# Adaptive-norm tables and S5 tables of a hybrid decoder step computed between the tiles of its first projection

## What is computed

```python
# adaLN: shift, scale and gate vectors from the conditioning row (9 rows: 1 prompt, 8 samples)
mod = jax.nn.silu(c) @ w_ada + b_ada            # (9,1024) @ (1024, 6*1024); w_ada_final: (1024, 2*1024)
sh1, sc1, gt1, sh2, sc2, gt2 = jnp.split(mod, 6, axis=-1)
h = rmsnorm(x, g_norm1) * (1.0 + sc1) + sh1     # x: 1088 tokens x 1024
proj = h @ w_in                                 # u is its first 512 columns; then q, k, v, forget gate
...
# S5, a diagonal complex state-space model over u: 32 groups of 16 channels, 64 states each
a = exp(lambda * dt); bb = f(a, lambda) * b
h_t = a * h_{t-1} + bb u_t;  y_t = Re(c h_t) + d u_t
...
# then attention, the output projection, and a mixture of experts (64 experts, top 6)
```

## Time and profile before

| | us |
|---|---|
| median of three runs (lowest, highest) | 2054.55 (2053.19, 2056.24) |
| the profiled execution, its own time | 2055.19 |
| the span that its trace covers | 2053.5 |
| PE busy in the span | 1815.0 (88%) |
| DVE busy | 851.8 (41%) |
| ACT busy | 451.1 (22%) |
| POOL busy | 218.3 (11%) |
| HBM read / written | 336.11 MB / 63.75 MB |

### The profile page before, as it was taken

The page is one execution under the profiler, slowest core; times in us unless marked ns, Lnnn a source line. Parts: engine busy times, 40 slices in busy tenths (PEclk is TensorE's granted clock), DMA queues, the critical chain, the costliest instruction groups (busy, mean ns, idle before and its releaser), DMA issues.

```text
span 2053.5 us, 25239 instructions
## 1 busy us (share of the span) xinstructions
PE 1815.0 (88%) x8920; PEld 942.0 (46%) x8920; DVE 851.8 (41%) x2392; ACT 451.1 (22%) x859; POOL 218.3 (11%) x183
## 2 busy tenths in 40 slices
PE   4568878999988887789888889999999999999985
PEld 1146555454445555455464334444444444444442
DVE  4943471003156555222236234344344434434438
ACT  0122213100044443130342111111111111111122
POOL 0000001000010000400000012222222222222210
PEclk7679958999978888899988989999999999999998
DMA  7932023000201003730017279999999999999666
GB/s 275 371 96 79 25 77 137 0 0 0 82 9 42 1 1 125 267 134 0 1 62 210 72 305 368 373 372 381 381 371 377 380 376 349 354 379 374 210 171 259
DMA packets 108585, 402.95 MB, mean 196 GB/s; under 512 B 27568, under 2 KB 38484, under 8 KB 78749
## 3 DMA queue, kind: packets, MB, share of 16 engines
q1 hardware_dynamic: 89452, 332.13, 42.2%
q0 software_dynamic: 19008, 69.21, 12.8%
HBM read 336.11 MB, written 63.75 MB: 195 GB/s over the span
## 4 chain that ended last, share of the span: by engine, by line
PE 47%; issue 6%; DVE 2%; DMA 1%; ACT 1%; POOL 0%; SPq 0%; POOLq 0%; DVEq 0%; ACTq 0%
PE psum L1033 22%; PE psum L1044 11%; PE psum L885 6%; PE psum L1012 3%; PE psum L1051 1%; PE psum L915 1%; PE psum L921 1%; PE psum L911 1%; PE psum L963 1%; PE psum L928 1%; DVE arena L1754 1%; DMA arena<-h_rows,arena 0%; DVE arena L1740 0%; DVE arena L1742 0%; DMA arena<-moe_rows 0%
## 5 line engine op out<-in xcount | busy, mean ns | idle before, releaser
L1033 PE MATMUL psum<-arena 128*32 128x512 f32 (+2 forms) x2016 | 464.4, 597 | 1.1 <-ACT arena L2019 1.1
L1033 PEld LDWEIGHTS psum<-arena 128*32 128x32 f32 (+2 forms) x2016 | 169.7, 139 | 241.7 <-issue 239.8
L1044 PE MATMUL psum<-arena,tail 128*32 128x512 f32 (+2 forms) x1000 | 231.6, 595 | 0.0
L1686 DVE TENSOR_TENSOR arena<-arena,psum 128x256 f32<-128x256 f32 x65 | 39.6, 609 | 339.4 <-ACT arena L2024 336.4
L2161 POOL DMA_INDIRECT moe_rows<-arena x64 | 101.6, 1588 | 576.0 <-DVE arena L1714 437.6
L1044 PEld LDWEIGHTS psum<-arena,tail 128*32 128x32 f32 (+2 forms) x1000 | 80.1, 138 | 105.1 <-issue 105.1
L703 PE MATMUL psum<-arena 128*128 128x512 f32 (+1 forms) x384 | 126.9, 494 | 0.0
L885 PE MATMUL psum<-arena 128*128 128x512 f32 (+1 forms) x288 | 124.3, 594 | 0.5 <-ACT arena L1950 0.5
L2024 ACT ACTIVATE arena<-psum 128x256 f32<-128x256 f32 x65 | 24.9, 383 | 445.0 <-PE psum L1033 445.0
L744 PE MATMUL psum<-arena 128*128 128x512 f32 (+2 forms) x192 | 89.9, 586 | 13.6 <-ACT arena L1868 13.6
L885 PEld LDWEIGHTS psum<-arena 128*128 128x128 f32 (+1 forms) x288 | 68.7, 239 | 54.8 <-issue 39.4
(11 more groups left out here) (488 smaller groups left out, 2251.0 us busy)
## 6 DMA issues: line engine op xcount, KB each, us to landing
arena<-in_w_exp_gate SPq DMA_DIRECT2D x66, 1024.0 KB, 19.2
arena<-in_w_exp_up SPq DMA_DIRECT2D x66, 1024.0 KB, 24.6
arena<-in_w_exp_down SPq DMA_DIRECT2D x66, 1024.0 KB, 21.6
arena<-in_w_ada SPq DMA_DIRECT2D x12, 2048.0 KB, 8.8
arena<-in_w_ada_final SPq DMA_DIRECT2D x4, 2048.0 KB, 8.5
arena<-in_cache_k SPq DMA_DIRECT2D x32, 256.0 KB, 4.4
arena<-in_cache_v SPq DMA_DIRECT2D x32, 256.0 KB, 3.9
arena<-moe_rows SPq DMA_DIRECT2D x16, 512.0 KB, 11.4
```

Source lines behind the costliest of these rows:

```text
L1033: ins = pe.matmul(slot[2 + par][lo:hi, :].rearrange("p (u n) -> p u n", u=2), xTs[:, par, k, lo:hi], gu, start=(k == 0), stop=(k == KD - 1))
L1044: ins = pe.matmul(slot[1][lo:hi, n * 512:(n + 1) * 512], hTs[:, k, lo:hi], down_ring[at][:, k * D + n * 512:k * D + (n + 1) * 512], start= ...
```

## The change

- Only the first adaLN group (pieces 0 to 3) and piece 4 are computed ahead of the u projection. Pieces 5 and 6 follow the transposes of tile 0, piece 7 the projection that is made in tile 1's turn, then 8, and one piece each (9 to 15) follows the projections in the turns of tiles 2 to 8. All groups now use PSUM slot 5, and all their transposes slot 4. The turns of groups 1, 2 and 3 stand in tile 1's turn, in tile 5's turn and behind the last projection.
- ACT's copies and bias additions of groups 1 to 3 stand between its norm and copy work of the tiles. The two sines of the rotation table now come behind the last of them.
- On DVE the two complex products are cut into halves of three operations each, and stand in the turns of tiles 1 to 4; the angles are cut into three parts in the turns of tiles 5 to 7. The scale `a1` is made ahead of the tiles, with only group 0 waited for; `a2` and `af` come after the skip term.
- BS and K come after UT on PE, and their copies after UT's on DVE. The DMAs of `M` come after them, so behind all loads of x and behind the eight small DMAs of the sample rows.
- The loads of x are interleaved with those of the weight pieces in SP's queue.
- ACT waits for `M`'s DMAs at the copy of S group 14, and no longer at the first tile of `u`. DVE waits for UTS ahead of writing the first states.
- Several arena offsets move (`u`, `u8`, `sq_junk`, `skip`).

The core of the diff, PE first:

```diff
+            ada_piece(0)
+            turn_parameters()
+            for n in range(1, NPIECE):
+                ada_piece(n)
+            turn_mod(0)
+            ada_piece(NPIECE)
...
+            for t in range(NT):
+                pe.wait_ge(xn_ready, t + 1)
+                fill(pe, ("X", t), t % 2)
...
+                full(ins, ("X", t))
+                if t == 0:
+                    ada_piece(5)
+                    ada_piece(6)
+                if t:
+                    project_u(t - 1)
+                    ada_piece(PIECE_AT[t])
+                if t == 1:
+                    ada_piece(8)
+                    turn_mod(1)
+                if t == 5:
+                    turn_mod(2)
+            project_u(NT - 1)
+            turn_mod(3)
```

DVE's loop over the tiles, then ACT's:

```diff
                     modulate(("X", t - 1), t - 1, slot[(t - 1) % 2], lambda k, t_=t - 1: tile_of(hT, t_, k), a1, lambda k: mod_t[:, k])
+                if t in (1, 2):
+                    output_table(t - 1)
+                elif t in (3, 4):
+                    input_table(t - 3)
+                elif t in (5, 6, 7):
+                    angles(t - 5)
```

```diff
-                    if t == 0:
-                        act.wait_ge(toeplitz, 16 * CH)
...
+                if t == 3:
+                    mod_out(1)
+                if t == 7:
+                    mod_out(2)
+                if t == 2:
+                    mod_copy(1)
                 if t >= 2:
                     u_out(t - 2)
+                if t == 5:
+                    mod_copy(2)
             u_out(NT - 2)
+            mod_copy(3)
             u_out(NT - 1)
+            mod_out(3)
...
                 full(act, ("S", gp))
+                if gp == 14:
+                    act.wait_ge(toeplitz, 16 * CH)
```

SP's queue (`load_x(t)` waits for the transposes of tile t-2):

```diff
+            for n in range(2, 5):
+                load_ada(n)
+            dma(w_u, ap["w_in"][0][:, 0:DA].rearrange("(k p) n -> p k n", p=P)).then_inc(ld["wu"], 16)
+            load_ada(5)
+            load_ada(6)
+            load_x(2)
+            for n in range(7, 9):
+                load_ada(n)
+            load_x(3)
+            load_ada(9)
+            load_ada(10)
+            for t in range(4, NT):
+                load_x(t)
+                load_ada(t + 7)
```

More of the change, by code:

```diff
@@ L565, in turn_mod @@
                 slots.wait_empty(pe, ("ADA", g))
-                fill(pe, ("ADT", g), 4 + g % 2)
+                fill(pe, ("ADT", g), 4)
                 for i in range(4):
-                    ins = pe.transpose(slot[4 + g % 2][:, i * P:(i + 1) * P], mod_row[:, g % 2, i * P:(i + 1) * P], ident)
+                    ins = pe.transpose(slot[4][:, i * P:(i + 1) * P], mod_row[:, g % 2, i * P:(i + 1) * P], ident)
                 full(ins, ("ADT", g))
[L571 to L586, removed]
@@ L587, in _, with ada_piece @@
-            turn_mod(NADG - 1)
+            def ada_piece(n):
+                g, q = divmod(n, NPIECE)
+                if q == 0:
+                    fill(pe, ("ADA", g), 5)
+                pe.wait_ge(ld_ada[n % 2], 16 * (n // 2 + 1))
+                for k in range(q * KPER, (q + 1) * KPER):
+                    for j in range(4):
+                        ins = pe.matmul(slot[5][32 * j:32 * (j + 1), :], cs_t[:, k, :], ada_w[:, n % 2, k % KPER, j * 512:(j + 1) * 512], start=(k == 0), stop=(k == KD - 1))
+                if q < NPIECE - 1:
+                    ins.then_inc(ada_used, 1)
+                else:
+                    full(ins, ("ADA", g))
@@ new lines, in _, with project_u @@
+            ada_piece(0)
[4 more added lines that the diff above has]
+            ada_piece(NPIECE)
+            def project_u(t):
+                slots.wait_empty(pe, ("X", t))
+                if t == 0:
+                    pe.wait_ge(ld["wu"], 16)
+                fill(pe, ("U", t), 2 + t % 2)
+                for k in range(KD):
+                    ins = pe.matmul(slot[2 + t % 2][0:rows(t), :], tile_of(hT, t, k), w_u[:, k, :], start=(k == 0), stop=(k == KD - 1))
+                full(ins, ("U", t))
@@ L590, in _ @@
+            project_u(NT - 1)
+            turn_mod(3)
+            slots.wait_empty(pe, ("U", 7))
+            for q in range(8):
+                fill(pe, ("UT", q), 4 + q % 2)
+                for i in range(4):
+                    ins = pe.transpose(slot[4 + q % 2][:, i * P:(i + 1) * P], u[:, 4 * q + i].rearrange("p t i -> p (t i)"), ident)
+                full(ins, ("UT", q))
             pe.wait_ge(s5_mats, 2)
```

178 lines of the change are left out of this document (88 added, 90 removed).

## The result

The changed kernel takes 1995.01 us, the median of four runs (1994.54 to 1997.38), against 2054.58 of the kernel before (2053.19 to 2056.24): 59.6 us less. The ratio worked out from the single runs is 0.9718, 95% interval 0.9697 to 0.9739 (the quotient of the two medians is 0.9710). Its profiled execution took 1995.10 us, with a span of 1993.4.

A forecast was written before the change was run, and what follows sets the result against it. The opening up to the first Y was bound by a weight-waiting and a PE-bound stage in sequence; its parts summed to Y at 208.2 instead of 258.43, 50.2 us less, giving 2004.3 us, range 2001 to 2018.

The forecast's parts named there:

- Part 2: Tile 1's turn, through tile 2's transposes: 17.0 us, ending at 84.7, with transposes at 1.84 and first projection 8.92.
- The bound: Opening up to first Y: a weight-waiting stage, then a PE-bound one, stand one after the other; first Y at 258.43.
- Part 1: Start up to weight piece 6: nothing changes, and piece 6 ends at 67.7.
- The upper bound of 13.6: First projection in tile 1's turn if wholly at the low clock; upper end of its -2 to +4.7 us.
- Part 3: Tiles 2 to 8: DVE sets the pace, PE's turn being 9.8; modulation of tile 7 ends at 146.7, PE at 163.4.
- Part 4: Ahead of UT: PE waits for ACT's group 3 bias additions, 2.64 and 0.1; UT starts at 166.2.
- Part 5: Behind the tiles: UT 5.7, BS 6.8, K 11.31 ending at 190.0, S to Y 15.59; Y starts at 208.2.
- the patchy clock: Rival: in the tiles' turns the high clock comes and goes, lengthening projections by 2.6; 2014 us, chance 0.17.
- Late weights: Rival: weight pieces inside the tiles' turns land late again, only piece 9 showing, +3; 2007 us, chance 0.04.
- the low clock throughout: Rival: interleaved tiles and pieces keep PE at 1.2 GHz, turns of 19.1; 2081 us, slower, chance 0.03.
- `M` was last: Rival: ahead of Y, the last `M` DMA lands after 7.7, ready at 211.9; 2008 us, chance 0.06.
- the sign that I had named: At the first Y: release by ACT's copy of S group 14 would show the forecast wrong.

The follow-up runs named there:

- turn_angles_late: turn_late with the last third of DVE's angles moved from tile 7's turn to behind the last modulation; ratio to the kernel before 0.9715.
- turn_late: The changed kernel with group 3's turn moved from ahead of UT to behind it; ratios to the kernel before 0.9698 and 0.9714.
- weights_first: The changed kernel with all weight pieces, their copies and turns ahead of the tiles again, x loads behind them; ratio to the kernel before 1.0093.
- after_delay1: The changed kernel with SP's first DMA held back by one GpSimd memset of 3.5 us; ratio to the kernel before 0.9751.

## Why the prediction was right and where it failed

The kernel took 1995.0 us for 2004.3 forecast. What failed is a size in two places, and not the mechanism. The transposes of tile 1 and the first projection (Part 2) were put at 10.76 us and took 8.24. And the difference that one run has from another was put at nothing: S took 7.68 us and not 9.10, and the part behind Y came out 4 us shorter, with attention's extent.

**The bound, and that two stages could share one stretch: right.** The first Y products stand in this order: 275.0 with only the tables between the tiles, 258.4 before, 250.6 with only the weights, 242.2 with neither (BS, K and `M` behind), 202.4 with all. Counted from 242.2, the weights alone cost 8.4 us, the tables alone 32.8, and both together gain 39.8. Neither part is good by itself, with BS, K and `M` behind the tiles in all four: DVE's tables and the weight stream must run at the same time as each other, as they did before, and the tiles must run beside both.

**Part 1: right**, 67.4 for 67.7 (66.0 and 67.4 in the other two traces of the changed kernel: in one of them piece 6 took 1.92).

**Part 2: the term that was mis-sized.** I took tile 1's transposes at 1.84 and the first projection at 8.92, both from tiles 0 and 1 of the kernel before, where PE had been idle ahead of them (3.78 and 1.12). In the changed kernel pieces 5 and 6 run right up to them, and they took 1.09 and 7.15. That is 2.5 of the 3.1 us of this step; the rest is overlap at the joints of PE's stages, which I had counted at full length. In all eight traces in which pieces and tile 1's transposes ran right up to the first projection it took 7.15. In the four in which PE had been idle shortly before (3.78 to 6.58 us, then tile 0's and tile 1's transposes, then another 1 us) it took 8.92, 7.26, 9.37 and 7.26. I had named 7.0 as the lower bound of this term, -2, and it came. Piece 7 in the earlier trace rows had shown the high clock behind two pieces, but the eight pieces after it in that trace took 2.62 to 3.64, each behind an idle span; what should have moved the forecast is that the change takes these spans away. (The upper bound of 13.6 doesn't follow from the words beside it: 3.64 for four steps is 0.91 a step, so 14.6 for sixteen. No run shows a projection wholly at the low clock.)

**Part 3: right in each term and in its end; the pace in between was PE's.** The turns of DVE were 14.4, 11.0, 12.2, 11.1 and 9.9 against 14.5, 11.1, 12.3, 11.3 and 10.0. DVE worked from 81.39 to 142.7 with no idle span over 0.33 us, and the projection of tile 7 began at 142.72, right behind its modulation, as forecast; the 4.0 us by which it was early are mostly those of Part 2. But PE, with its backlog from tile 1's turn, ran at its own 9.87 up to the projection of tile 5, and waited for DVE only 1.6 us in all. So the forecast tile periods of 11 to 12.5 us, with transposes released by DVE, were not seen (PE's were 9.87, then 10.9, 11.1 and 9.9). The two ways of counting end 1.6 us apart, and turn_angles_late showed how little relieving DVE gives (0.16 us).

**Part 4, the new wait: right.** 2.74 predicted, 2.85 in the trace; turn_late took it away.

**Part 5: mostly right.** K as computed; UT took 0.6 us more and BS 1.2 less than put. The stretch from S to Y was 1.2 us shorter: S ran at 7.68 instead of the 9.10 of the earlier trace rows, with a granted clock of 1.00 for 0.87. This differs from run to run: S took 9.10 and 10.26 in the kernel before, 7.68, 9.35 and 7.68 in the changed one, and in the ten traces with BS and K behind the tiles it was four times 7.7 and six times 9.0 to 10.0. Whether the change makes the short one more frequent isn't shown. One reading was wrong: I wrote that only DVE's last quarter needs the copies of S groups 14 and 15. The first Y products need the slot that S group 14 holds, so they too wait for `M` and one copy.

**The rivals.** The clock stayed at 1.00 over the tiles; the patchy clock didn't occur in the changed kernel, but did in weights_first (0.89). The Trainium skill's rule on cycling through PSUM ("TensorE: Matmul & The Clock Gate", section "A second HAM failure mode: psum-queue depth-cycling") was weighed as a reason for it; here a handover every 2 to 7 us with dense work on both sides did not bring it about (clock 1.00), and it came in weights_first, in two turns with longer waits. Late weights and the low clock throughout did not occur. `M` was last after all, by under 0.2 us: Y was released by ACT's copy of S group 14, the sign that I had named, in the four traces in which S took 7.7 (two of the three of the changed kernel, after_delay1, turn_angles_late), and by DVE in the others. It cost nearly nothing, since `M` was ready at 201.8 and not at the 211.9 of that rival; but where S is short, `M`'s DMAs are now the limit of this place.

**The range: too narrow at its low end.** The sum's own range began 3 us below the forecast. It had one term with a lower bound, and none for the lengths taken from a stretch with a partly low clock (S), for joints counted twice, nor for what a run may differ in. Attention alone moves by 6.6 us between traces of one kernel. Between the profiled executions, 2005.0 forecast and 1995.1 measured, lie 9.9 us: 5.8 ahead of Y, 4 behind it, where the first trace of before had attention's long extent and that of after the short one. The medians lie 59.6, 57.7 and 56.4 us below those of the kernel before in the three comparisons; the three ratios of the changed kernel, 0.9718, 0.9723 and 0.9725, give 57 us, which is the saving at Y (56.1 in the first pair of traces, 57.6 in the second: 259.2 and 201.6). So, as far as intervals of 4 to 9 us can tell, the saving reached the end whole, as forecast, and none of it comes from behind Y.

## What to carry to other kernels

Put stages with different limits beside each other all at once, and count which engine each part needs: here, with BS, K and `M` behind the tiles, moving the weights alone between the tiles lost 8 us at the first Y product, the tables alone lost 33, and both together gained 40. When a matrix product is moved behind other matrix work, take its length from a row at the clock that it will then have, not from its old place behind an idle stretch. Before asking what saved the last few us, trace the unchanged kernel a second time.

## What the runs showed of the hardware

- The attention stage of one program, the kernel before, took 198.7 us in one execution and 205.3 in another, with two patterns of the granted clock; programs that differ only ahead of it took these or 202.3. The S stage of 128 small products took 9.10 and 10.26 us in the kernel before, 7.68 to 10.03 in the others. The time of the kernel before moved over 15 to 17 us between executions on one chip, more than the runs at the start (3 us) had let me think.
- In turns in which PE waited 3.7 us (2.24 and 1.48) and 5.2 us (4.46 and 0.76) the next projection took 9.65 and 9.27 instead of 7.26, and the clock over the tiles was 0.89; behind 3.3 us (1.77 and 1.55) it took 7.26. With a piece of 1.92 us in each turn it was 1.00, and the projections took 7.15 to 7.26. Idle time ahead did not always cost: behind 6.57 and 1.12 us one first projection still took 7.26.
